# A two-block transformer kernel on one core: the first input in five parts, matmuls of a ones tile ahead of it, the constants later, the first norm's sums and spread two slots on

## The reference, cut to what matters

```python
def _rmsnorm(x, g):
    xf = x.astype(jnp.float32)
    y = xf * lax.rsqrt(jnp.mean(xf * xf, axis=-1, keepdims=True) + EPS)
    return (y * g.astype(jnp.float32)).astype(x.dtype)
...
    for i in range(DEPTH):                       # DEPTH = 2
        hn = _rmsnorm(h, norm_g[i])
        u = hn @ w_in[i]
        a_val, a_glu, a_z, q, k, v, b_z = jnp.split(u, offs, axis=-1)
        ya = _conformer_conv(a_val, a_glu, conv_w[i], conv_b[i], cln_g[i], cln_b[i])
        ...
        h = h + jnp.concatenate([ya, yb], axis=-1) @ w_out[i]
        e = _rmsnorm(p[i] @ w_pe[i], pe_g[i])
        h = h + e * jax.nn.sigmoid(h @ w_pg[i])
    return _rmsnorm(h, final_g)
```

## Time and profile before

| | us |
|---|---|
| median of 3 runs | 1775.32 |
| the three runs | 1775.28, 1775.32, 1788.3 |
| the profiled execution | 1777.53 |
| its span in the profile | 1775.7 |
| PE busy | 1752.4 |
| DVE busy | 1309.9 |
| ACT busy | 899.9 |

### The profile page before, as it was taken

The page is one execution under the profiler, slowest core; times in us unless marked ns, Lnnn a source line. Parts: engine busy times, 40 slices in busy tenths (PEclk is TensorE's granted clock), DMA queues, the critical chain, the costliest instruction groups (busy, mean ns, idle before and its releaser), DMA issues.

```text
span 1775.7 us, 35754 instructions
## 1 busy us (share of the span) xinstructions
PE 1752.4 (99%) x14377; PEld 1670.2 (94%) x14377; DVE 1309.9 (74%) x2087; ACT 899.9 (51%) x1326; POOL 40.3 (2%) x48
## 2 busy tenths in 40 slices
PE   8999999999999999999999999999999999999997
PEld 7999999999999999999999899998989999999876
DVE  7899799977679987998776765555565656666754
ACT  5343665545533455546465463545455443655653
POOL 0000000000000000000000110100100000000000
PEclk9999999999999999999999999999999999999999
DMA  7676545555666664456555656665655666455553
GB/s 233 190 209 189 190 144 175 193 191 192 197 188 205 195 199 145 146 190 201 189 191 186 204 180 210 189 189 176 201 157 169 196 188 189 140 158 170 173 189 130
DMA packets 200082, 326.07 MB, mean 184 GB/s; under 512 B 14911, under 2 KB 66319, under 8 KB 199821
## 3 DMA queue, kind: packets, MB, share of 16 engines
q1 hardware_dynamic: 197085, 320.85, 57.9%
q10 hardware_dynamic: 2864, 3.36, 0.6%
HBM read 320.42 MB, written 2.69 MB: 182 GB/s over the span
## 4 chain that ended last, share of the span: by engine, by line
PE 81%; DVE 12%; issue 2%; ACT 2%; DMA 1%; SPq 1%; ACTq 1%; DVEq 0%
PE g L495 62%; PE g L506 11%; DVE w_lo L912 5%; DVE cacc L1158 4%; PE att L629 2%; PE att L650 2%; PE att L605 2%; DMA turned<-q 1%; ACT w_hi L1541 1%; ACTq L1529 0%; DVE u L1006 0%; SPq L308 0%; PE att L495 0%; PE att L803 0%; SPq L286 0%
## 5 line engine op out<-in xcount | busy, mean ns | idle before, releaser
L912 DVE TENSOR_TENSOR w_lo<-stage,w_hi 128x1024 fp32r<-128x1024 f32 x577 | 705.6, 1231 | 385.6 <-ACT w_hi L1541 384.8
L1541 ACT CAST w_hi<-stage 128x1024 fp32r<-128x1024 f32 x577 | 598.7, 1050 | 588.6 <-PE g L495 367.0
L495 PE MATMUL g<-a_hi,w_hi 128*128 128x256 f32 x2496 | 700.7, 281 | 3.2 <-DVE w_lo L912 1.9
L495 PE MATMUL g<-a_lo,w_hi 128*128 128x256 f32 x2496 | 691.9, 277 | 0.0
L495 PE MATMUL g<-a_hi,w_lo 128*128 128x256 f32 x2496 | 691.9, 277 | 0.0
L495 PEld LDWEIGHTS g<-a_hi,w_hi 128*128 128x128 f32 x2496 | 469.4, 188 | 12.8 <-issue 10.0
L495 PEld LDWEIGHTS g<-a_lo,w_hi 128*128 128x128 f32 x2496 | 469.7, 188 | 0.0
L495 PEld LDWEIGHTS g<-a_hi,w_lo 128*128 128x128 f32 x2496 | 469.0, 188 | 0.4 <-issue 0.2
L495 PE MATMUL g<-b_hi,w_hi 128*128 128x256 f32 x1440 | 401.9, 279 | 1.3 <-DVE w_lo L912 1.2
L495 PE MATMUL g<-b_hi,w_lo 128*128 128x256 f32 x1440 | 399.0, 277 | 0.0
L495 PE MATMUL g<-b_lo,w_hi 128*128 128x256 f32 x1440 | 399.0, 277 | 0.0
(11 more groups left out here) (232 smaller groups left out, 1375.6 us busy)
## 6 DMA issues: line engine op xcount, KB each, us to landing
stage<-in_fox_w_in_dram SPq DMA_DIRECT2D x128, 512.0 KB, 3.8
stage<-in_w_in_dram SPq DMA_DIRECT2D x112, 512.0 KB, 3.8
stage<-in_swa_w_in_dram SPq DMA_DIRECT2D x72, 512.0 KB, 3.9
stage<-in_w_in_dram SPq DMA_DIRECT2D x128, 256.0 KB, 3.1
stage<-in_w_out_dram SPq DMA_DIRECT2D x64, 512.0 KB, 4.3
stage<-in_w_pg_dram SPq DMA_DIRECT2D x64, 512.0 KB, 4.1
stage<-in_fox_w_out_dram SPq DMA_DIRECT2D x32, 512.0 KB, 4.5
stage<-in_swa_w_out_dram SPq DMA_DIRECT2D x32, 512.0 KB, 4.2
```

The costliest lines, as they stand in the source:

```text
L495: mm = pe.matmul(acc[:, j * S:(j + 1) * S], w[:, slot, c0 + j * P:c0 + (j + 1) * P], xx[:, k, :], start=st and m == 0 and j % 2 == 0, stop ...
L912: dve.tensor_tensor(w_lo[:, slot, :], stage[:, slot, :], w_hi[:, slot, :].bitcast(F32), ALU.subtract).then_inc(*t.inc("w_split"))
L1541: act.copy(w_hi[:, slot, :], stage[:, slot, :]).then_inc(*t.inc("w_rounded"))
```

## The change

- **x in five parts** instead of four: channel groups 0-1, 2-3, 4-7, 8-11, 12-15 (parts 0 to 4). Parts 0 to 3 are issued ahead of pieces 0 to 3, part 4 ahead of piece 5, the constants ahead of piece 6 (before: ahead of piece 4).
- **Turning x**: parts 0 and 1 (4 transposes each) before the first matmul, part 2 in slot 0, part 3 in slot 4, part 4 in slot 9 of chunk 0; the constants in slot 13 (before 11). PE waits for the first `a_lo` of parts 0, 1, 2, 3, 4 at pieces 0, 1, 2, 4, 6.
- **Matmuls of the ones tile** (`warm`): 8 before the gains are turned, 4 after part 1 of x; nothing reads their result.
- **The first norm**: `stats` in slot 4 and `spread_rs` in slot 8 of chunk 1 (before 2 and 6).
- **Hooks**: on ACT x part 3 and square 0 after cast 4, square 1 after cast 5, x part 4 after cast 6, square 2 after cast 7, square 3 after cast 8. On DVE x part 3 after split 4, x part 4 after split 6, add 0 after split 7, add 1 after split 8, the constants and add 2 after split 9, add 3 after split 10.

```diff
+        X_PARTS = ((0, 2), (2, 4), (4, 8), (8, 12), (12, 16))
...
-                        before = {g: x_part(g) for g in range(4)} | {4: consts}
+                        before = {0: x_part(0), 1: x_part(1), 2: x_part(2), 3: x_part(3), 5: x_part(4), 6: consts}
...
-                    if ready and n % 2 == 0:
+                    if ready and (n % 2 == 0 or ready == "parts" and n == 1):
                         pe.wait_ge(*t.see("operand_ready"))
...
-                    if g >= 2:
+                    if g >= 3:
                         pe.wait_ge(*t.again("h_new", 1))
...
+            def warm(n):
+                for _ in range(n):
+                    pe.matmul(OB[:, 0:P], ones[:, :], ones[:, :], start=True, stop=True)
...
+            pe.wait_ge(*t.again("ones_set"))
+            warm(8)
             pe.wait_ge(*t.see("ident_in", 16))
             turn_gains()
             turn_x(0)()
             turn_x(1)()
-            pe.wait_ge(*t.again("ones_set"))
+            warm(4)
...
-                chunk("T", A, p0, ready=True, work={15: [stats()]} if l else {3: [turn_x(2)], 5: [turn_x(3)], 11: [turn_consts]})
-                chunk("T", A, p1, work={3: [spread_rs()]} if l else {2: [stats()], 6: [spread_rs()]})
+                chunk("T", A, p0, ready=True if l else "parts",
+                      work={15: [stats()]} if l else {0: [turn_x(2)], 4: [turn_x(3)], 9: [turn_x(4)], 13: [turn_consts]})
+                chunk("T", A, p1, work={3: [spread_rs()]} if l else {4: [stats()], 8: [spread_rs()]})
...
             x_low(0)()
             x_low(1)()
             split()
+            x_low(2)()
+            split()
             x_new(0)()
-            x_new(1)()
-            split()
-
-            tail = {1: [x_low(2), x_new(2)], 2: [x_low(3), x_new(3)],
-                    4: [add_squares(0)], 5: [consts, add_squares(1)], 6: [add_squares(2), add_squares(3)]}
+
+            tail = {1: [x_low(3), x_new(1)], 2: [x_new(2)], 3: [x_low(4), x_new(3)], 4: [add_squares(0)],
+                    5: [add_squares(1)], 6: [consts, add_squares(2)], 7: [add_squares(3)]}
...
-            tail = {1: [x_high(2)], 2: [x_high(3)], 3: [h_wait, square(0, h)],
-                    4: [h_wait, square(1, h)], 5: [h_wait, square(2, h)], 6: [h_wait, square(3, h)], 7: [rel_table]}
+            tail = {1: [x_high(3), h_wait, square(0, h)], 2: [h_wait, square(1, h)], 3: [x_high(4)],
+                    4: [h_wait, square(2, h)], 5: [h_wait, square(3, h)], 7: [rel_table]}
```

More of the change, by code:

```diff
@@ L220, in two_blocks, with x_bank @@
         ACC = {0: G[0], 1: G[1], "S": AA[:, 0:2 * CH], "O": AA[:, 2 * CH:4 * CH]}
-        def x_bank(g, n):
+        def x_bank(k):
+            g, n = divmod(k, 4)
             return ((G[1][:, (n // 2) * CH:(n // 2 + 1) * CH], (SB, TB)[n // 2])[g % 2])[:, (n % 2) * S:(n % 2 + 1) * S]
@@ L231, in two_blocks @@
         names = """w_rounded w_split w_used gemm_free operand_ready
[L232 removed]
+            dve_step act_step pool_step x_in0 x_in1 x_in2 x_in3 x_in4 gains_in gains_turned gains_done x_turned consts_in consts2_in tables_in rel_ready rel_out rel_bias_done
             bias_in scored s_free maxed weights_ready pt_done t_free att_done normed ob_free mb_free
@@ L301, in go @@
                 def go():
-                    cols = slice(g * CH, (g + 1) * CH)
+                    cols = slice(X_PARTS[g][0] * P, X_PARTS[g][1] * P)
                     sp.dma_start(u[:, :].rearrange("p (b d) -> p b d", b=NB)[:, :, cols],
@@ L676, in go @@
                     pe.wait_ge(*t.see(f"x_in{g}", 16))
-                    if g >= 2:
+                    if g >= 3:
                         pe.wait_ge(*t.again("h_new", 1))
-                    for n in range(4):
-                        dst = x_bank(g, n)
+                    for k in range(*X_PARTS[g]):
+                        dst = x_bank(k)
                         for b in range(NB):
-                            k = 4 * g + n
                             mm = pe.transpose(dst[:, b * P:(b + 1) * P], u[:, b * D + k * P:b * D + (k + 1) * P], ident[:, :])
                     mm.then_inc(*t.inc("x_turned"))
-                    t.skip("h_new")
-                return go
+                    if X_PARTS[g][1] % 4 == 0:
+                        t.skip("h_new")
+                return go
+            def warm(n):
+                for _ in range(n):
+                    pe.matmul(OB[:, 0:P], ones[:, :], ones[:, :], start=True, stop=True)
             def turn_gains():
@@ L1087, in go @@
                     dve.wait_ge(*t.see("x_turned"))
-                    for n in range(4):
-                        k = 4 * g + n
-                        if n % 2 == 0:
+                    for k in range(*X_PARTS[g]):
+                        if k % 2 == 0:
                             dve.wait_ge(*t.see("x_rounded", 2))
-                        dve.scalar_tensor_tensor(out=XY[0][1][:, k, :], in0=x_bank(g, n), scalar=gains[:, 0, k:k + 1],
+                        dve.scalar_tensor_tensor(out=XY[0][1][:, k, :], in0=x_bank(k), scalar=gains[:, 0, k:k + 1],
                                                  in1=XY[0][0][:, k, :].bitcast(F32), op0=ALU.mult,
-                                                 op1=ALU.subtract).then_inc(*t.inc("operand_ready" if n == 3 else "dve_step"))
+                                                 op1=ALU.subtract).then_inc(*t.inc("operand_ready" if k == X_PARTS[g][1] - 1 else "dve_step"))
                 return go
@@ L1632, in go @@
                     act.wait_ge(*t.see("x_turned"))
-                    for n in range(4):
-                        k = 4 * g + n
-                        f_(XY[0][0][:, k, :], x_bank(g, n), ACT.Copy, "x_rounded", scale=gains[:, 0, k:k + 1])
+                    for k in range(*X_PARTS[g]):
+                        f_(XY[0][0][:, k, :], x_bank(k), ACT.Copy, "x_rounded", scale=gains[:, 0, k:k + 1])
                 return go
@@ L1642, in _ @@
             rounded()
+            x_high(2)()
             rounded()
```

## The result

The changed kernel takes 1799.24 us, the median of four runs. One of them was disturbed; the other three lie between 1795.79 and 1801.59. The kernel before took 1776.29 beside it (1775.28 to 1788.3). The ratio is 1.0105, 95% interval 1.0079 to 1.0131. Fastest against fastest the difference is 20.5 us, where 4.1 had been forecast. The profiled execution took 1801.59 us, with a span of 1799.8.

A forecast was written before the change was run, and what follows sets the result against it. PE bounds the kernel, with DVE close behind: PE alone 2.0 us later, `rs` copied 4.1 later, and the end moves by 4.1. Profiled 1777.53 to 1781.6, median 1779.4; own range 1778.3 to 1780.4, wider range 1774.5 to 1782.5.

The forecast's parts named there:

- The start: First L495 matmul on PE at 9.6 us instead of 11.16, 1.56 earlier, because part 0 of x is smaller.
- The last turn of x: PE turns part 4 in slot 9 at 24.9 us, so DVE's norm work starts 4.4 us later than before.
- Piece 6 came late: Rival: piece 6 arrives after 23.4 us, costing 1 us for each beyond its 1.3 spare; 0.06 together with anything else.
- DVE blocked by squares 2 and 3: DVE idles 2.1 us after add 0 and again after add 1, waiting for a square and a cast on ACT.
- PE's waits at pieces 9 and 10: PE waits 2.0 us for split 9 and 1.9 us for split 10.
- `rs`: DVE's copy of `rs` in the first norm comes at 53.5 us instead of 49.37, 4.1 later.
- DVE catches PE up near 94 us, so that the end moves by this: DVE has no slack after copying `rs`, so its 4.1 us delay, not PE's own 2.0, reaches the end.
- kept: Rival, chance 0.12: ACT and DVE don't block each other at squares 2 and 3; start gain stays, 1773.6 us.
- made up: Rival, chance 0.13: DVE makes up its lag, so only PE's own 2.0 us counts, 1777.3 us.
- The clock low at the first matmuls: Rival, chance 0.09: first matmuls run partly at half rate after PE idles, +4.8 to +5.3 us, 1780.4.
- Both ends for all twelve: 0 to 0.2; I take 0.: At PE's start, the twelve ones matmuls are hidden at full rate and cost 0.2 us at half rate.
- no case reaches 1%: Whole kernel: no case reaches the 17.8 us that can be told from no change; same 0.98, slower 0.01.

The follow-up runs named there:

- wide ones: The changed kernel with the ones work at the start as 3 matmuls of 512 columns instead of 12 of 128; ratio to before 1.0033.
- thin ones: The changed kernel with its twelve ones matmuls cut from 128 columns to one; median 1799.97 us, ratio to before 1.0122.
- before with 6 and with 18 thin ones: The kernel before with 6 or 18 one-column ones matmuls added ahead of the gains; ratio 1.0048 with 6, one run of 1786.59 us with 18.

## Why the prediction was wrong

- **The start**: forecast 9.6, measured 9.53, and 9.38 without the ones. There they cost 0.15 us, within the 0 to 0.2 of the bound.
- **The last turn of x**: forecast 24.9, measured 25.22. Piece 6 came late, cast 6 at 24.79 instead of 23.4. That used up the 1.3 us to spare and no more: the gain of part 4 begins at 26.29, after a wait for PE's turn.
- **DVE blocked by squares 2 and 3**: forecast 2.1 twice, measured 2.12 twice. With the squares moved back both are gone.
- **PE's waits at pieces 9 and 10**: forecast 2.0 and 1.9, measured 1.35 and 1.42. Both were too large by about half a microsecond, because PE came later: its matmuls stood 0.118 us apart here, not 0.1134. It cost nothing, since the split decides when PE goes on: forecast 15.7 and 20.3 after the last turn of x, measured 15.72 and 20.23.
- **`rs`**: forecast 53.5, measured 53.97. **DVE catches PE up near 94 us, so that the end moves by this**: right, and PE alone was 2.2 us late before it, where 2.0 was forecast; most of the catching up came earlier, from 71 to 79 us. The changed kernel with wide ones has just this and no stop; it is 5.1 us slower by the fastest runs, 5.9 by the ratio, against 4.1 forecast. The two rivals "kept" and "made up" fell.
- **The clock low at the first matmuls**: didn't happen, but only because of the ones. I had set it aside because before stayed at full rate, with sixteen transposes ahead. Without ones, or with thin ones, the matmuls behind the eight that are left run at half rate, and `rs` comes 2.2 and 2.9 us later. The row of before was luck in part: before with 6 and with 18 thin ones has sixteen transposes too, and some 16 and 21 of its first matmuls of piece 0 stand 0.21 us apart. By the Trainium skill's rule ("TensorE: Matmul & The Clock Gate", Part 4), which says transposes don't count, the run without ones agrees, and the kernel before doesn't: there the second eight got faster (1.64 us after 1.97) with nothing but transposes and one small matmul ahead.
- **What failed is the sentence "Both ends for all twelve: 0 to 0.2; I take 0."** I bounded the ones matmuls by their own duration at their own place. They measured about 16 us (20.5 against 5.1 with the same columns in 3 matmuls, 16.7 when added alone to the kernel before), all of it at the loop's two jumps back. From the first matmul of one turn to that of the next there are 105.35 us (1106.15 to 1211.50), before 97.50 (1094.67 to 1192.17): 7.9 for a jump, two stops and the matmuls at half rate together. The sum also took the full rate behind them as given, which without them would have failed by 2.2 us of `rs`. I also wrote that no case reaches 1%, and the ratio is 1.0105; none of my rivals could act outside the first 100 us.

Could it have been foreseen? The trace of before has 94 instruction packets in all and 3 from 1050 to 1250 us, though the loop comes round twice there. The loop ran from code that was already held, and this could be lost. Its size would not have come out of that, but a rival of "some microseconds at each jump back" could have.

## What to carry to other kernels

An instruction added to a program that loops has a second price besides its time: it moves the code of every loop behind it. Here 6 to 12 matmuls at the start cost 7 to 17 us at the two jumps back of one loop, and nothing at the shorter loop behind it. When a small edit moves the time by more than it can explain, compare the instruction queue's packets of the two profiles, and look at how long the loop's branch takes and at the first matmul behind each jump; then change the count of instructions alone, before any reason is looked for in the data. Fewer, wider instructions for the same work (3 of 512 columns for 12 of 128) kept the loop where it was good.

## What the hardware showed that I had not expected

- Code of a loop is fetched anew or not by its place: 94 packets or 112, and the pattern comes back after 256 recorded instructions (64 matmuls of ones). The branch takes 4.5 to 5.8 us instead of 0.2, PE has two stops of 1.8 to 4.0 us (6 thin: one), and where it stops twice the granted clock is 0.50 for some 4 us.
- A one-column fp32 matmul of ones takes as long as a wide one at the start: the timeline has 8 of them in 3.58 us with one column, against 3.41 with 128. With one column they didn't raise the rate: behind 64 of them, 27.47 us, the first eight transposes still took 1.97 us.
- The same row of matmuls has two speeds at a granted clock of 1.00, 113.4 and 117.8 ns for one, over stretches of up to 126 us. It goes with differences of 4 to 9 us between executions of one kernel, and it stays open.
